# Expert token rows kept in their own column order, with the gather reading stationary columns at a step of eight

## What is computed

```python
x = _layernorm(DEEPNORM_ALPHA * x + h, post_ln[l, 0, 0], post_ln[l, 0, 1])
x = _layernorm(DEEPNORM_ALPHA * x + _moe(x, router_w, router_b, moe_w_gate[l], moe_w_up[l], moe_w_down[l]),
               post_ln[l, 1, 0], post_ln[l, 1, 1])

def _moe(x, router_w, router_b, w_gate, w_up, w_down):
    ...                     # sigmoid scores, the best group of four experts, the two best in it: gates
    for e in range(N_EXPERTS):
        h = jax.nn.silu(xt @ w_gate[e]) * (xt @ w_up[e])
        y = y + gates[:, e:e + 1] * (h @ w_down[e])
```

## Time and profile before

| | |
|---|---|
| median of 3 runs | 1263.17 us (1260.47 to 1266.61) |
| the profiled execution, its own time | 1261.89 us |
| its span, first to last instruction | 1260.2 us |
| TensorE (PE) busy | 1097.6 us, 87% |
| weight loads (PEld) busy | 754.7 us, 60% |
| DVE busy | 572.6 us, 45% |
| ACT busy | 364.7 us, 29% |
| mean granted TensorE clock, of full speed | 0.941 |
| gather matmuls, xtm_hi and xtm_lo | 192 and 192 |

### The profile page before, as it was taken

The page is one execution under the profiler, slowest core; times in us unless marked ns, Lnnn a source line. Parts: engine busy times, 40 slices in busy tenths (PEclk is TensorE's granted clock), DMA queues, the critical chain, the costliest instruction groups (busy, mean ns, idle before and its releaser), DMA issues.

```text
span 1260.2 us, 23437 instructions
## 1 busy us (share of the span) xinstructions
PE 1097.6 (87%) x10165; PEld 754.7 (60%) x10166; DVE 572.6 (45%) x1066; ACT 364.7 (29%) x733; POOL 63.1 (5%) x98
## 2 busy tenths in 40 slices
PE   3999858899978859999999799989888599999994
PEld 3999557799955654444443499976646544444442
DVE  5654945655547463222222664485433632222225
ACT  2444613443321241111110433463232411111102
POOL 1011100011000000000000101121100000000000
PEclk9999958999997969999999899999878699999997
DMA  9502200011022817999999901554742279999991
GB/s 301 214 14 58 75 1 3 3 37 37 24 81 97 332 76 313 420 421 422 420 422 418 386 23 67 178 202 157 271 174 89 86 310 421 421 420 421 422 415 47
DMA packets 55035, 273.97 MB, mean 217 GB/s; under 512 B 5153, under 2 KB 5418, under 8 KB 29842
## 3 DMA queue, kind: packets, MB, share of 16 engines
q1 hardware_dynamic: 45570, 237.96, 46.9%
q0 software_dynamic: 9360, 34.46, 8.7%
HBM read 265.98 MB, written 6.46 MB: 216 GB/s over the span
## 4 chain that ended last, share of the span: by engine, by line
PE 77%; DVE 14%; ACT 3%; issue 2%; DVEq 2%; DMA 2%; SPq 0%; POOLq 0%; ACTq 0%; POOL 0%
PE ps L698 71%; DVE arena L2059 1%; DVE arena L2072 1%; ACT arena L1366 1%; PE ps L804 1%; PE ps L1255 1%; DMA arena<-in_cache_k 1%; DMA arena<-in_x_sample 1%; PE ps L1107 1%; PE ps L1008 1%; ACT arena L1369 0%; DVE arena L1870 0%; DVEq L1819 0%; ACT pw_hi L1366 0%; PE ps L1112 0%
## 5 line engine op out<-in xcount | busy, mean ns | idle before, releaser
L698 PE MATMUL ps<-arena 64*64 64x64 f32 (+14 forms) x7320 | 634.6, 321 | 65.9 <-DVE arena L1837 17.1
L698 PEld LDWEIGHTS ps<-arena 64*64 64x64 f32 (+5 forms) x7320 | 355.0, 142 | 327.2 <-issue 249.0
L1369 ACT COPY arena<-ps 128x512 f32<-128x512 f32 (+7 forms) x291 | 119.6, 432 | 388.4 <-PE ps L698 180.3
L2072 DVE TENSOR_TENSOR arena<-arena,ps 128x512 f32<-128x512 f32 x16 | 17.1, 1069 | 173.8 <-PE ps L698 173.8
L2081 DVE SCALAR_TENSOR_TENSOR yy_lo<-ps,arena,yy_hi 128x512 fp32r<-128x512 f32 x32 | 22.5, 746 | 114.1 <-ACT yy_hi L1366 114.1
L1366 ACT ACTIVATE arena<-ps,arena 128x256 f32<-128x256 f32 (+5 forms) x96 | 46.2, 507 | 81.6 <-PE ps L698 50.0
L1366 ACT ACTIVATE pw_hi<-arena 128x1024 fp32r<-128x1024 f32 x40 | 41.9, 1056 | 91.1 <-PE ps L698 83.5
L698 PE MATMUL ps<-px_hi,pw_hi 128*128 128x336 f32 x192 | 63.0, 328 | 2.3 <-DVE px_lo L1962 1.3
L698 PE MATMUL ps<-px_lo,pw_hi 128*128 128x336 f32 x192 | 61.4, 320 | 0.0
L698 PE MATMUL ps<-px_hi,pw_lo 128*128 128x336 f32 x192 | 61.3, 319 | 0.0
L698 PE MATMUL ps<-yy_hi,sg 128*128 128x512 f32 (+1 forms) x96 | 46.7, 487 | 16.5 <-DVE arena L2059 11.4
(11 more groups left out here) (220 smaller groups left out, 1447.1 us busy)
## 6 DMA issues: line engine op xcount, KB each, us to landing
arena<-in_moe_w_gate SPq DMA_DIRECT2D x64, 1024.0 KB, 13.9
arena<-in_moe_w_up SPq DMA_DIRECT2D x64, 1024.0 KB, 17.2
arena<-in_moe_w_down SPq DMA_DIRECT2D x64, 1024.0 KB, 11.7
arena<-in_rwkv_w_rkv SPq DMA_DIRECT2D x6, 2048.0 KB, 18.9
arena<-in_w_kv_shared SPq DMA_DIRECT2D x4, 2048.0 KB, 19.7
arena<-in_cache_k POOLq DMA_DIRECT2D x16, 512.0 KB, 4.4
arena<-in_cache_v POOLq DMA_DIRECT2D x16, 512.0 KB, 7.1
arena<-in_rwkv_w_out SPq DMA_DIRECT2D x2, 2048.0 KB, 11.5
```

Of the source, the lines that this page charges most:

```text
L698: return pe.matmul(out, lhsT, rhs, start=start, stop=stop)
L1369: return act.copy(out, in_)
L2072: tt(HH.rearrange("p (k q) -> p q k", k=NF), HS.rearrange("p (q k) -> p q k", k=NF), bank(3).rearrange("p (q k) -> p q k", k=NF), ALU.mult ...
```

## The change

The split no longer reorders: ACT copies and DVE subtracts plain rows, and `XTM` keeps the column order of `YT`. The order is made by the gather: its stationary operand for block c is now the columns c, c + 8, c + 16, ... (`c:D:NC`, a step of 8 elements or 32 bytes) instead of 128 neighbours. Column p of it is feature 8p + c as before. The overflow branch's gather does the same.

```diff
@@ gather
-                            m = mm(ps[:, i % 2, QUAD * (c % 2):QUAD * (c % 2) + QUAD], XTM[h][t][0:k, P * c:P * c + P],
+                            m = mm(ps[:, i % 2, QUAD * (c % 2):QUAD * (c % 2) + QUAD], XTM[h][t][0:k, c:D:NC],
                                    SelF[q % 2][0:k, t].rearrange("p e s -> p (e s)"), t + h == 0, t + h == 3)
@@ more_block
-                            m = mm(ps[:, c // 4, P * (c % 4):P * (c % 4) + P], XTM[h][t][0:k, P * c:P * c + P],
+                            m = mm(ps[:, c // 4, P * (c % 4):P * (c % 4) + P], XTM[h][t][0:k, c:D:NC],
                                    SelO[0:k, t, :], t + h == 0, t + h == 3)
@@ normed_copy
-                f(XTM[0][t][0:n, :].rearrange("t (k p) -> t p k", k=NC), YT[0:n, t, :].rearrange("t (p k) -> t p k", k=NC),
-                  ACT.Copy).then_inc(S("xtm_hi"), 1)
+                f(XTM[0][t][0:n, :], YT[0:n, t, :], ACT.Copy).then_inc(S("xtm_hi"), 1)
@@ remainder
-                    lo, hi = [XTM[h][t][0:n, :].rearrange("t (k p) -> t p k", k=NC) for h in (1, 0)]
-                    tt(lo, YT[0:n, t, :].rearrange("t (p k) -> t p k", k=NC), hi.bitcast(F32), ALU.subtract).then_inc(S("xtm_lo"), 1)
+                    tt(XTM[1][t][0:n, :], YT[0:n, t, :], XTM[0][t][0:n, :].bitcast(F32), ALU.subtract).then_inc(S("xtm_lo"), 1)
```

## The result

The changed kernel takes 1311.53 us (median of 4 runs, 1305.64 to 1318.36) against 1263.43 us before (4 runs, the three of the table above and one more): a ratio of 1.0382, 95% interval 1.0322 to 1.0443. It is slower by 48.1 us. The forecast was 1299 us with a range up to 1308, so the direction was right and the size too small: the median lies 3.5 us above the range.

The account below looks back on a forecast made before the run. TensorE was taken to bound the kernel. Slower gather loads, +37.4 us, less 1.3 us for the third subtraction, gave +36.1 on 1261.89, or 1298.0; with the median 1.3 above that execution, 1299 us, range 1258 to 1308.

Parts of the forecast that it names:

- What bounds the kernel: MoE expert pairs, 29.70 us each: TensorE bounds them, DMA is not waited for, so a longer gather finds no cover.
- What paces a gather: Gather matmuls start 0.120 us apart at the matmul's own pace; weight loads alone would take 0.112, leaving 0.008 us of room.
- What a step costs: Gather weight loads: 1.73 ns a stepped column against 0.83, so 0.227 us a matmul; 350 matmuls pay 37.4 us.
- The matmuls at the lower clock: First 17 matmuls of each layer's first gather, at 1.2 GHz: stepping adds at most 0.3 us over 34, left out.
- The clock: Rival: clock falls in all twelve gathers inside pairs, slowing following expert matmuls, 1.8 us each, 21.6 us, 1321 us; chance 0.07.
- The gain: Split copies get cheaper; only the third subtraction is on the path before the gather, saving 0.67 us a layer, 1.3 in all.
- The free step: Rival: gather weight loads keep 0.83 ns a column whatever the step, leaving only the -1.3 us, 1262 us; chance 0.28.
- Two passes: Rival: an fp32r weight load reads its columns twice, paying the step on both, about 1385 us; chance 0.04.

## Why the prediction came out as it did

**What bounds the kernel: right.** No wait hid the longer gathers. Every nanosecond of the load beyond 0.120 us is in the pair's chain: 24 x (0.242 - 0.120) = 2.93 us, and the run of 132 grew from 24.42 to 27.35 wherever no fall came on top. DMA got its slack, 348 to 415 GB/s in the pairs instead of 421.

**What paces a gather: right.** The load had 8 ns of room. With 64 stepped columns, half the load, the starts were 0.125 us apart, 5 ns over the plain pace.

**What a step costs: the right mechanism, the term mis-sized.** The sum put a stepped column at 1.73 ns, from one DVE read and two writes; it is 1.85 for a load. That makes the pace 0.242 us instead of 0.227 and the 350 matmuls 42.7 us instead of 37.4. The row of another engine gave the mechanism and came within 7%, but a sum over 384 repeats needs the row of the engine itself. This term alone, with the next one, would have given 1305 us, still inside the range.

The Trainium skill, page "Advanced Engine Details and Errata", section "SBUF Cachelines", had the rule: lines of 16 bytes, two hits on each to hide the access. By that rule the trace agrees in every step tried: steps of 1 and 2 fp32 elements are at the plain price within 5 ns, steps of 4 to 8 pay in full, 0.32 to 0.34 us, and a step of 3 lies between at 260. The Trainium skill's rule in "TensorE: Matmul & The Clock Gate", section "LDWEIGHTS (loading the stationary operand)", that only the number of columns counts, holds for steps of 1 and 2 and fails at a step of 8 (338 ns against 191).

**The matmuls at the lower clock: a step that failed, small.** The sum let the first 17 matmuls of a first gather off, on the ground that a plain load takes 1.67 ns for a column there. They paid (0.242 - 0.214) x 34 = 1.0 us. The text's own bound of 0.3 us came from the same 1.73. In layer 0 the clock also came back later than before, 8.0 us after the gather's start instead of 3.6; to stepped loads that made no difference.

**The clock: the step that failed, and what put the time outside the range.** It was set down as a rival in which all twelve gathers fall, at 0.07, and left out of the forecast and of the range. In the profiled execution the clock fell in seven of the twelve; four falls outlasted the gather and cost 1.76 to 2.08 us each, near the 1.8 us that the rival had priced, and three ended inside the gather and cost nothing: 7.6 us. The mistake was to treat as all or nothing what comes and goes from pair to pair. With the price and the mechanism at hand, some falls should have been in the likeliest case, and the upper end of the range at least at 1321. The reason given against it was that the gather streams seven times as many columns for a load as the router. It is 256 against 16, sixteen times for a load, and in time about eight or nine (256 in 0.227 us, 16 in 0.112 to 0.136); either way the router was the wrong row to compare with. The run with seven more small matmuls for each block (six falls) and the one with 512 moving columns (none) show that the slower pace of the gather itself was enough.

**The gain: right.** The third subtraction took 1.21 us instead of 1.89, and the way from the scores to the gather became shorter by 0.66 us in both layers (11.31 and 11.26 us instead of 11.97 and 11.92); the run with that step moved away altogether got most of the rest. The first two stayed covered; DVE just waits longer for the scores (2.72 us instead of 1.45 in layer 0).

**The rivals.** The free step is out (338 ns). Two passes at the full price are out (they would be above 500 ns). The forecast of 1299 plus the dearer column (5.3), the matmuls at the lower clock (1.0) and the falls (7.6) is 1313, against 1311.53 measured. That it comes so close is partly luck: the falls are counted in one execution of the four, which took 1308.80 us, and the same terms put that one at 1311.9; the other three took 1305.64 to 1318.36 us at mean clocks of 0.932 to 0.918, and how many of their gathers fell is not known. (A slip that changes nothing: +36 us on 1263 is +2.8%, not +2.9%.)

## What to carry to other kernels

If a layout must be reordered, ask of every reader and writer how many elements it takes from each 16 bytes, not how far it steps: here runs of two fp32 elements cost next to nothing on ACT, DVE and the weight load (6% at most, on ACT), while single elements make them 1.6 to 1.9 times as long. Put a remaining step where it is paid six times (the split) and not 384 times (the gather), and check beforehand how close the weight load is to the matmul's pace, here 8 ns. When a stream of matmuls gets slower without more columns, count on the clock falling in some of its passes, look in each for whether the fall outlasts the part that does not depend on the clock, and put that into the range.

## What the runs showed of the hardware that I had not expected

- A stepped weight load does not follow TensorE's clock: 338 ns at 1.2 and at 2.4 GHz, where a plain one takes 330 and 191.
- The price goes by the 16-byte lines touched, 1.8 to 1.9 ns each: 0.173 us between loads for 96 lines (step 3), 0.227 to 0.242 for 128. Among steps of 4 to 8 it varies by 7% and not in order: 5 is the cheapest (0.227), then 6 (0.23), 4 and 7 (0.233 to 0.235), 8 (0.242).
- A clock fall in a slowed gather of plain loads cost 4.8 us a pair (about 10 us at 1.2 GHz), in a gather of stepped loads 1.8 to 2.1 (about 6.8 us at 1.2 GHz, of which only the 3.5 to 4 us behind the gather count) or nothing (about 3.4 us, all inside the gather).
